# Decay arguments of a two-way state-space scan, moved from VectorE to ScalarE in a fused encoder block

## What is computed

```python
ac = (dt * A).reshape(b, nc, CHUNK, g, h).transpose(0, 3, 4, 1, 2)
a_cum = jnp.cumsum(ac, axis=-1)
Lmat = jnp.exp(segsum(ac))             # exp(a_cum[i] - a_cum[j]) for j <= i, else 0
cb = jnp.einsum('bclgn,bcsgn->bgcls', Cc, Bc)
y_diag = jnp.einsum('bgcls,bghcls,bcsghp->bclghp', cb, Lmat, xc)
decay_states = jnp.exp(a_cum[..., -1:] - a_cum)
states = jnp.einsum('bclgn,bghcl,bclghp->bcghpn', Bc, decay_states, xc)
y_off = jnp.einsum('bclgn,bcghpn,bghcl->bclghp', Cc, states, jnp.exp(a_cum))
```

## Time and profile before

| | |
|---|---|
| median of 3 runs (lowest to highest) | 1587.81 us (1587.65 to 1588.23) |
| the profiled execution: its time | 1587.99 us |
| its span, first to last instruction | 1586.3 us |
| TensorE busy in the span | 1533.9 us (97%) |
| VectorE busy | 1016.3 us (64%) |
| ScalarE busy | 727.2 us (46%) |
| mean granted TensorE clock | 0.991 of full |

### The profile page before, as it was taken

One profiled execution on the slowest core, in us unless ns is written; L12 is line 12 of the kernel. 1 busy time (PEld: TensorE's weight loads), 2 busy tenths in 40 slices (PEclk: granted clock), 3 DMA queues, 4 the chain that ended last, 5 costly groups with the idle time before them and its releaser, 6 DMA issues.

```text
span 1586.3 us, 25891 instructions
## 1 busy us (share of the span) xinstructions
PE 1533.9 (97%) x9501; PEld 1374.6 (87%) x9501; DVE 1016.3 (64%) x1553; ACT 727.2 (46%) x851; POOL 24.2 (2%) x29
## 2 busy tenths in 40 slices
PE   6999999898999999999999999999999999999998
PEld 6999888886788888888889998899988998889987
DVE  5889899999976666565556555455554555545553
ACT  4355555454664544544344443434433444334432
POOL 0000000000101000000000000000000000000000
PEclk9999999999999999999999999999999999999999
DMA  8875556555565666565556655566556665656552
GB/s 255 253 221 175 142 177 169 161 181 175 160 191 174 184 174 185 175 233 175 193 186 179 183 183 196 177 182 178 193 192 177 183 186 191 194 165 183 186 196 95
DMA packets 186338, 291.60 MB, mean 184 GB/s; under 512 B 13533, under 2 KB 67151, under 8 KB 185984
## 3 DMA queue, kind: packets, MB, share of 16 engines
q1 hardware_dynamic: 183748, 285.92, 59.5%
q10 hardware_dynamic: 2492, 4.36, 0.9%
HBM read 288.04 MB, written 5.34 MB: 185 GB/s over the span
## 4 chain that ended last, share of the span: by engine, by line
PE 77%; DVE 14%; issue 5%; DVEq 1%; ACT 1%; DMA 0%; ACTq 0%
PE psum L1142 75%; DVE w_lo L748 3%; DVE mix L774 3%; DVE conv L794 2%; DVE mix L765 2%; DVE cbm L805 1%; DVE xbc L799 0%; DMA x_in<-in_x 0%; PE psum L1241 0%; PE psum L1261 0%; ACT w_hi L463 0%; PE psum L1187 0%; DVE gate_t L812 0%; ACT conv_t L490 0%; DVE conv L790 0%
## 5 line engine op out<-in xcount | busy, mean ns | idle before, releaser
L748 DVE TENSOR_TENSOR w_lo<-raw,w_hi 128x1024 fp32r<-128x1024 f32 x512 | 624.8, 1223 | 457.6 <-ACT w_hi L463 454.0
L463 ACT ACTIVATE w_hi<-raw 128x1024 fp32r<-128x1024 f32 x512 | 540.5, 1057 | 734.9 <-PE psum L1142 732.2
L1142 PE MATMUL psum<-actT_lo,w_hi 128*128 128x256 f32 x1792 | 514.6, 287 | 11.8 <-DVE w_lo L748 11.8
L1142 PE MATMUL psum<-actT_hi,w_hi 128*128 128x256 f32 x1792 | 510.6, 285 | 0.0
L1142 PE MATMUL psum<-actT_hi,w_lo 128*128 128x256 f32 x1792 | 510.5, 285 | 0.0
L1142 PEld LDWEIGHTS psum<-actT_lo,w_hi 128*128 128x128 f32 x1792 | 347.7, 194 | 20.4 <-DVE w_lo L748 13.2
L1142 PEld LDWEIGHTS psum<-actT_hi,w_lo 128*128 128x128 f32 x1792 | 347.6, 194 | 0.2
L1142 PEld LDWEIGHTS psum<-actT_hi,w_hi 128*128 128x128 f32 x1792 | 347.4, 194 | 0.0
L1142 PE MATMUL psum<-w_hi,hid_lo 128*128 128x512 f32 x512 | 199.2, 389 | 0.0
L1142 PE MATMUL psum<-w_lo,hid_hi 128*128 128x512 f32 x512 | 199.2, 389 | 0.0
L1142 PE MATMUL psum<-w_hi,hid_hi 128*128 128x512 f32 x512 | 199.2, 389 | 0.0
(11 more groups left out here) (188 smaller groups left out, 1124.5 us busy)
## 6 DMA issues: line engine op xcount, KB each, us to landing
raw<-in_w_in SPq DMA_DIRECT2D x128, 512.0 KB
raw<-in_w_up SPq DMA_DIRECT2D x128, 512.0 KB
raw<-in_w_down SPq DMA_DIRECT2D x128, 512.0 KB
raw<-in_w_out SPq DMA_DIRECT2D x64, 512.0 KB
raw<-in_w_in SPq DMA_DIRECT2D x64, 256.0 KB
raw<-in_w_in SPq DMA_DIRECT2D x128, 128.0 KB
decay<-decay_rows SPq DMA_DIRECT2D x16, 512.0 KB, 5.2
rel_tiles<-rel_rows ACTq DMA_DIRECT2D x1, 3072.0 KB, 19.5
```

The lines of the kernel that those rows point to most:

```text
L463: act.activation(w_hi[j % RING][:, :, :], raw[j][:, :, :], ACT.Copy).then_inc(hi_ready, 1)
L748: tt_(w_lo[i][:, :, :], raw[j][:, :, :], w_hi[i][:, :, :].bitcast(f32), ALU.subtract).then_inc(lo_dve, 1)
L1142: return pe.matmul(o, lhsT, rhs, start=first, stop=last, **kw)
```

## The change

The decay arguments move from VectorE to ScalarE, and so do their slots: head 0 to slot k = 6, head 1 to 7, head 2 to 9 and head 3 to 11 (before: 8, 9, 10, 11). Within a chunk ScalarE writes Relu of the negated sum, with the negated columns in a new tile `tokn`, and `head_exp` takes the exponential with scale -1; since relu(-x) is -min(x, 0), the value is the same. Across chunks the argument is never positive there, so that no minimum is taken: one exponential with the column as its bias gives the result at once. `head_exp` is two instructions of 128x256 in place of one of 128x768. Ahead of the loop VectorE makes `tokn` once. The scripts of the other steps stand as they were.

```diff
+ARG_SLOTS = {6: 0, 7: 1, 9: 2, 11: 3}
...
+        tokn = place("tokn", [P, 2, 64])
...
+            def decay_args(G, h):
+                H, w = 4 * G + h, mix[h]
+                act.wait_ge(decay_in, 32 * (G + 1))
+                act.wait_ge(y_done, H + 1)
+                f, b = ds(H, 1), ds(32 + H, 1)
+                for k, d, l, src, col in ((0, 0, 0, 0, f), (2, 0, 1, 1, f), (3, 1, 0, 0, b), (5, 1, 1, 1, b)):
+                    act.activation(w[:, k, :], decay[:, d, h, P * l:P * l + P], ACT.Relu,
+                                   bias=tokn[:, src, col], scale=-1.0)
+                act.activation(w[:, 1, :], decay[:, 0, h, P:2 * P], ACT.Exp, bias=tokp[:, 2, f])
+                act.activation(w[:, 4, :], decay[:, 1, h, 0:P], ACT.Exp, bias=tokp[:, 2, b]).then_inc(args_ready, 1)
...
-                act.activation(mix[h][:, :, :], mix[h][:, :, :], ACT.Exp).then_inc(decays_ready, 1)
+                act.activation(mix[h][:, 0:3:2, :], mix[h][:, 0:3:2, :], ACT.Exp, scale=-1.0)
+                act.activation(mix[h][:, 3:6:2, :], mix[h][:, 3:6:2, :], ACT.Exp, scale=-1.0).then_inc(decays_ready, 1)
...
+                    if k in ARG_SLOTS and (i == 0 or more):
+                        decay_args(G + 1, ARG_SLOTS[k])
                     if k == 10:
...
+                if s - GROUP_SLOT[1] in ARG_SLOTS:
+                    act.wait_ge(m1_free, 1)
+                    decay_args(0, ARG_SLOTS[s - GROUP_SLOT[1]])
...
-            def decay_args(G, h):
-                H, w, rows = 4 * G + h, mix[h], decay
-                dve.wait_ge(decay_in, 32 * (G + 1))
-                dve.wait_ge(y_done, H + 1)
-                f, b = ds(H, 1), ds(32 + H, 1)
-                for k, (d, l, src, col) in enumerate((
-                        (0, 0, 0, f), (0, 1, 2, f), (0, 1, 1, f), (1, 0, 0, b), (1, 0, 2, b), (1, 1, 1, b))):
-                    ins = ts_(w[:, k, :], rows[:, d, h, P * l:P * l + P], tokp[:, src, col], 0.0, ALU.add, ALU.min)
-                ins.then_inc(args_ready, 1)
...
-                if 8 <= k < 12:
-                    decay_args(G, k - 8)
...
+                ts_(tokn[:, :, :].rearrange("p a h -> p (a h)"), M1[:, 0:128], -1.0, None, ALU.mult)
```

## The result

The changed kernel takes 1591.09 us (median of 12 runs, 1589.01 to 1592.28), the kernel before 1588.22 us (median of 12). The ratio is 1.0017, with a 95% interval from 1.0009 to 1.0024: slower by 1.4 to 3.8 us. I had forecast 1582.6 us, so the step that was to bring 5 us is missing, and some 3 us more are lost.

A forecast was written before the change was run, and what follows sets the result against it. VectorE was taken to set the pace in the scan windows, with ScalarE nearly as late. Exchange -0.2 and turn -5.1 sum to -5.3 us on 1587.99, 1582.7; median 0.2 lower, so 1582.6 us, range of 8 in 10 1579 to 1591.

The forecast's parts named there:

- ScalarE's step (0.30 us): One 128x128 step with a column as bias on ScalarE: 0.30 us, six a head 1.8 us, bounds 1.2 and 2.5.
- The dear step of 0.41: Rival: ScalarE's step costs 0.41 us as wider rows do, adding 9.8 us over seven chains, 1592.4 us; chance 0.08.
- The chain of an even group: From the gate's end (T) through ScalarE and VectorE: slot 12 begins at T + 14.8 instead of 14.4, losing 0.4 us.
- The odd group: Same chain without `conv_in`: slot 12 at T + 13.9 where it was 14.5, gaining 0.6 us.
- the exchange: Moving the steps between the two queues, four even and three odd groups: -0.2 us, worth nothing.
- The turn (-5.1 us): VectorE's scan loop, shortened from 413 to 311 instructions, stops refetching code: two turns give back 2.54 us each.
- my own sign of a wrong forecast: The forecast is wrong if VectorE's "issue" idle time at the turn stays, among other signs.
- slower, by code fetches: Rival: code kept depends on where a body lies; ScalarE's 221 and VectorE's MLP loop stall, 1595.3 us; chance 0.11.
- SyncE's 258: Argument against code-fetch stalls: SyncE's MLP turn of 258 instructions crosses two boundaries of 128 and turns at once.
- the turn stays as it is: Rival: 311 instructions are still too long for VectorE's scan loop, 1587.6 us; chance 0.17.
- The Trainium skill's rule against relu on ScalarE: Relu, max, min and add belong on VectorE; weighed at 1.17 us a head there against 1.8 on ScalarE.

The follow-up runs named there:

- shift_70: The changed kernel with 70 instructions that do nothing at the head of VectorE's program; 1583.25 us, ratio 0.9965.
- a_unroll: The changed kernel with VectorE's scan windows 1 to 3 written out three times instead of a hardware loop of 311 instructions; 1582.34 us, ratio 0.9961.
- written out: VectorE's scan windows 1 to 3 as straight code instead of a hardware loop, no turn: kernel before 1582.24 us, changed kernel 1582.34 us.
- shift_64: The changed kernel with 64 instructions that do nothing at the head of VectorE's program; 1582.94 us (one run).
- before_47: The kernel before, its VectorE scan turn 413 instructions, with 47 instructions that do nothing at the head of VectorE's program; 1588.20 us (one run).
- a_early: The changed kernel with ScalarE's arguments of heads 2 and 3 moved ahead of the gate's squaring (k = 8); 1577.62 us, ratio 0.9936.
- a_hide: The changed kernel, but heads 2 and 3 on VectorE: head 2 between the gate and `sq_lo`, head 3 behind `sq_lo`; 1574.41 us, ratio 0.991.
- a_split: The changed kernel, but heads 2 and 3 on VectorE at k = 10 and 11, ahead of slots 11 and 12; 1583.81 us, ratio 0.9973.
- shift_96: The changed kernel with 96 instructions that do nothing at the head of VectorE's program; 1583.50 us (one run).

## Why the prediction was wrong

- **ScalarE's step (0.30 us): right.** Head 2 takes from 222.84 to 224.60, 1.76 us for six steps, 0.29 each; I had 1.8. The dear step of 0.41 is out.
- **The chain of an even group: right.** `rnorm` ends at 229.11, T + 9.4 (forecast 9.35); slot 12 begins at T + 14.95 (forecast 14.8, though its terms as printed add up to 14.7). Only the wait was less than I said: `newton` waits 2.24 us, not some 4, over seven groups 15.6, since VectorE has already waited 1.21 us for the `w_hi` ahead of head 2.
- **The odd group: right where there is no turn** (13.94, forecast 13.9). Without turns the exchange came out at +0.1 us (forecast -0.2).
- **The turn (-5.1 us): the step that failed.** I took a body's length as what decides, and 311 as nearer to 258 than to 413. The idle time stayed, which was my own sign of a wrong forecast, and the same 311 instructions pause at two of five places and turn freely at the other three. My rival "slower, by code fetches" had the right thought in it, that what is kept is counted from where a body lies, but put it on ScalarE's 221 and on the MLP loop, which turned in 0.28 and 0.3 us as before. The argument by which I held it down, SyncE's 258, was sound for 258: a body within 259 covers three pieces from nearly every place. For 311 it said nothing.
- **The turn's price: missed.** My rival "the turn stays as it is" names what happened, but not its reason, for 311 isn't too long as such; and in it I took the pause as the same wherever it stays (1587.6). In the kernel before, 1.17 us of subtractions lay queued behind the branch and covered a part of it; the change removed them. Idle time at the two turns rose from 2.72 + 2.54 to 3.18 + 2.87 us, 0.8 in all. By the medians the turns cost 7.8 (`shift_70`) or 8.8 us (`a_unroll`) instead of 5.9, but not all of that is the turns'.
- **Where the rest of the loss lies.** From the end of group 0's gate to the end of group 7's, the profiled executions take 301.9 us before and 295.2 written out, 302.8 changed and 295.8 in `shift_70` or 294.6 written out: 6.7 us for the turns before, 7.0 to 8.3 changed. Nor is the whole loss the scan's: the changed kernel is 1.5 us behind the kernel before at VectorE's first branches in the attention loop (515.3 against 513.8) and in the MLP's (1217.7 against 1216.2), and 2.9 us at the second one of the MLP's (1401.4 against 1398.5).
- **The clock.** I gave the gaps no price in TensorE's clock. A pause reaches TensorE as a wait for `mix`, 3.9 us in the kernel before (it ends at 293.4), 3.8 us in the changed kernel at about 291 to 295 us and 1.97 in `shift_64`, and the granted clock behind a long one is below full speed. Here are the kernel before, the changed kernel and `shift_64` (the column behind POOL's is the clock, as a share of 2.4 GHz), each from 286 to 305 us, the first two also in the MLP:

```profile
286.00:305.00 19.00, 15.11 (x103) 13.11 (x102) 18.65 (x40) 4.24 (x4) 0.00 (x0) 0.82 0.72 207
1218.00:1226.00 8.00, 7.30 (x60) 7.30 (x61) 5.42 (x6) 2.12 (x2) 0.00 (x0) 1.00 0.79 264
```

```profile
286.00:305.00 19.00, 15.20 (x112) 13.59 (x111) 18.29 (x38) 8.43 (x17) 0.00 (x0) 0.91 0.75 218
1218.00:1226.00 8.00, 5.83 (x36) 5.83 (x37) 5.58 (x7) 1.65 (x2) 0.00 (x0) 0.79 0.57 182
```

```profile
286.00:305.00 19.00, 15.06 (x121) 13.46 (x121) 17.20 (x33) 9.08 (x19) 0.00 (x0) 1.00 0.72 214
```

With the shorter gap the clock stays at its upper level in this stretch. It isn't safe for that: elsewhere in `shift_64` the clock is at its lower level, 1.2 GHz, behind a wait of TensorE for `sq_lo` of 1.98 us that ends at 218.9:

```profile
219.20:222.60 3.40, 3.40 (x18) 3.40 (x17) 2.55 (x3) 3.40 (x8) 0.00 (x0) 0.51 0.07 8
```

The second rows above, from the MLP, show another loss. There both kernels do the same work, and at the start of each turn TensorE waits for `w_lo`, 2.73 us in both. Behind this wait the changed kernel is at half clock for 3.4 us, in which it runs 18 matmuls, and the kernel before at full clock, with 29. The changed kernel's row is first, then that of the kernel before:

```profile
1220.80:1224.20 3.40, 3.40 (x18) 3.40 (x18) 2.72 (x3) 0.00 (x0) 0.00 (x0) 0.50 0.80 242
1218.80:1222.20 3.40, 3.40 (x29) 3.40 (x30) 3.25 (x3) 0.32 (x1) 0.00 (x0) 1.00 0.67 189
```

So its first full turn takes 183.7 us instead of 182.3. That is 1.4 of the 2.9 us between the two profiled executions. It isn't tied to the change: `before_47`, which does the same work as the kernel before, has a turn of 183.8, and `shift_64` one of 183.7, with its half clock from 1212.5 on. A third wait of this kind, 2.63 us at the MLP's first `w_lo`, has half clock behind it in the changed kernel and full clock in `shift_70`, which is 1.5 of the 7.7 us between their profiled executions:

```profile
1036.50:1039.90 3.40, 3.40 (x16) 3.40 (x17) 3.33 (x3) 0.00 (x0) 0.00 (x0) 0.50 0.60 172
1030.30:1033.70 3.40, 3.40 (x28) 3.40 (x29) 3.31 (x3) 0.26 (x1) 0.00 (x0) 1.00 0.63 179
```

The waits are equally long, so their length alone doesn't decide whether the clock falls; what does isn't shown here. Two kernels can differ by 1.5 us at each such place with no difference in their work.

The Trainium skill's rule against relu on ScalarE ("ScalarE: Activation LUTs", section "Rules for kernel authors"), which I had weighed, holds by the step (1.76 us a head against 1.17). It doesn't decide the kernel: `a_early` has all 24 steps of a group on ScalarE and gains 10 us over the kernel before, as they fill idle time there.

## What to carry to other kernels

Before a step is moved to a less busy engine, ask whether it stands on a chain that both engines share; there an exchange is worth nothing, and the same step in a slot where its engine waits is worth most of its length (`a_hide` and `a_split`, equal work: slot 12 comes 1.9 us earlier for 2.3 us of steps, and the kernels are 9.4 us apart). A loop's turn that stalls for code is seen in the sequencer's rows, branch to next instruction, and in the count of instruction packets; where the body is near the limit, try it at several places before calling its length the cause, and look for queued work that covers the pause and that an edit may take away. Before a difference of 1 to 3 us is put down to an edit, compare the stages that it doesn't touch.

## What the hardware showed that I had not expected

- VectorE's branch back is free (0.3 to 0.4 us) or costs 2.8 to 3.9 us of its sequencer's time, by where the body lies. All of VectorE's loops seen agree with one rule, in which the size of a piece and the place of the first body are inferred: free if the body lies within three pieces of 128 instructions. Free were 311 in 3 of 5 places (`shift_64`, `shift_70`, `shift_96`), 311, 291, 273 and 259 in other loops, 362 at one place; 311 at two, 362 at three and 413 at two paused. That a fourth piece is held by the code next ahead, which is fetched before the branch, would explain it, but is argued and not shown.
- 70 instructions that do nothing, at the head of VectorE's program, make the kernel 7.8 us faster; in the profiled executions some 6 of them are there by the end of the scan. A difference of half a per cent between two versions of a looped kernel may be that and nothing else.
- A relu with a scale of -1 and a column as bias on 128x128 costs 0.39 us alone and 0.29 in a row of its like on ScalarE; a 128x128 step of add and min with a column costs VectorE 0.21 (six in 1.26 us).
